# A two-layer hybrid encoder trunk: operands at equal addresses modulo 512 bytes, and the transposes of token blocks 0 and 1 moved to the end of each stage's tail

## The chip, the cores and the metric

The kernel runs on one core of one Trainium2 chip. The metric is the device time of one execution in microseconds, the median of three.

## The reference

Two layers work on 512 tokens of width 1024 in float32. Each layer is three sub-layers, each with an RMSNorm before it and one after it. What matters here:

```python
def swiglu(x, w_gate, w_up, w_down):
    return (jax.nn.silu(x @ w_gate) * (x @ w_up)) @ w_down
...
    for l in range(DEPTH):
        f = swiglu(rms_norm(x, ffn1_pre_g[l]), ...)        # 1024 -> 2816 -> 1024
        x = x + 0.5 * rms_norm(f, ffn1_post_g[l])
        m = hybrid_mixer(rms_norm(x, mix_pre_g[l]), ...)   # in-projection, MLA | GLA | retention, out-projection
        x = x + rms_norm(m, mix_post_g[l])
        f = swiglu(rms_norm(x, ffn2_pre_g[l]), ...)
        x = x + 0.5 * rms_norm(f, ffn2_post_g[l])
```

## The kernel before, in words

**Stages.** There are six stages: FFN, mixer, FFN in each layer, numbered 0 to 5 (`stage % 3 == 1` is a mixer). The program is written per engine, each engine in its own order, with semaphores between them. TensorE (PE) does the matmuls, ScalarE (ACT) and VectorE (DVE) prepare operands and evacuate, GpSimd (POOL) computes inverse roots, SyncE (SP) issues the loads of weights.

**Three matmuls for one.** For accuracy, each float32 operand is split in a high part (rounded to float32r by ACT) and a low part (the rest, by DVE). `three` (L405 to L408) multiplies high by high (L406), high by low (L407), low by high (L408).

**Weights.** They come as a stream of 1 MB "pairs" (two 128-row slabs): 33 for an FFN (`FFN_PAIRS`; 22 for gate and up, 11 for down; `FT` is 22), 12 for a mixer. SP loads pair p into `raw[:, p % 2]` once pair p-2 has been split. ACT's `high` or `high_next` (L838, L853) writes the high part into a slot, DVE's `lows` (L1125) the low part. `slot_of` says which slot: 0 and 1 are halves of `WH`/`WL`, 2 is `WH2`/`WL2`, 3 to 5 are `W3` to `W5`, which lie over `hL`. `high` waits until the slot's last user on PE is done (`pair_done`).

**Which operand is held.** Of a matmul's two operands one is loaded into the array (held, 128 columns), the other streams through (moved, 256 or 512 columns). In gate, up and in-projections a weight tile is held and `xH`/`xL` (the normed, transposed x) moves. In the down and out-projections a piece of `hH`/`hL` (or `xH`/`xL`) is held and the weights move.

**Addresses.** Tiles follow each other in each partition. `x`, `xH`, `xL`, `raw`, `WH`, `WL`, `WH2`, `WL2` start at 128 modulo 512 bytes. Behind a row of small tiles comes `small_end`, 32 bytes, and after it start `hH` and `hL`, and over them `norm_g`, `step`, `xn`, `squares`, `W4`, `W3`, `W5` and the mixer's tiles: the named ones at 0 modulo 512. Steps within all of these are multiples of 512 bytes.

**A tail and the next entry.** An FFN's down projection runs pair by pair over all 8 output tiles (`down_pair`), except for its last three pairs: `last_pairs` goes by token block b (128 tokens, two PSUM banks 2b and 2b+1), and within it over the three pairs n = 0, 1, 2, so that block 0 is complete after a quarter of these 144 matmuls; this stretch is called the tail here. The mixer's out-projection ends in the same way. For each block that is complete, the other engines go through a chain: ACT squares and sums the output (`square_f`, L861), DVE adds (`average_f`, L1144), POOL takes the inverse root (L1476), DVE scales and adds the residual (`residual`, L1153, L1155), ACT squares x (`square_x`, L873), DVE and POOL again (L1160, L1476), DVE writes the normed block to `xn` (`normed`, L1169), PE transposes it (`turn_block`, L418, eight transposes into banks 2b and 2b+1), ACT writes `xH` (`high_x`, L878) and DVE `xL` (`low_x`, L1174). The order in which ACT and DVE take these steps for the four blocks is written out in their two `enter` functions. PE's `turn_block` calls for blocks 0 and 1 stand inside the tail, ahead of n = 1 of b = 2 and b = 3. The next stage begins with `half_pair`: the first pair and the second pair over tokens 0 to 255 (which needs `xH` and `xL` of blocks 0 and 1), with the transposes of blocks 2 and 3 inside, and then both over tokens 256 to 511.

Of the kernel before, what the change touches and what calls it, by code (L numbers as in the profile page):

```python
# [21 lines left out]
P = 128  # L22
# [5 lines left out]
FT = FF // P  # L28
# [14 lines left out]
FFN_PAIRS = FT + FT // 2  # L43
# [5 lines left out]
STAGES = 3 * DEPTH  # L49
# [47 lines left out]


def slot_of(stage, i):
    if i < 2:  # L100
        return 2 + i
    if stage % 3 == 1:
        return {10: 4, 11: 5}.get(i, i % 2)
    return 4 if i == FFN_PAIRS - 1 else i % 2


def first_pair_of(stage):
# [4 lines left out]
def hybrid_trunk(nc, x_in, positions, stream, gains_in, norm_gains, w_q_up, w_kv_up, w_gate_up, b_gate, consts, out):  # L112
    ctx = ExitStack()
    with ctx:
        def sb(name, shape, dt=F32, stack=ctx):
            return stack.enter_context(nc.sbuf_tensor(name, shape, dt))
# [60 lines left out]
        share = sb("share", [P, 2, BLK])  # L177


        sb("small_end", [P, 8])  # L180
        with ExitStack() as hidden:
            hH = sb("hH", [P, FT, SEQ], F32R, hidden)
            hL = sb("hL", [P, FT, SEQ], F32R, hidden)
# [75 lines left out]
        pair_done = sem("pair_done", 0)  # L259
# [139 lines left out]
        def _(pe):  # L399
# [34 lines left out]
            def enter(stage, base, widths=(P, P)):  # L434

                if stage == 0:
                    turn_block(0, 0)
                    turn_block(0, 1)
                wait_pair(base)
                pe.wait_ge(xH_ready, BLK * stage + 2)  # L440
                pe.wait_ge(xL_ready, BLK * stage + 2)
                lower = half_pair(2, (0, 1), 0, (P, P), {})
                if stage:

                    lower.then_inc(pair_done, 1)
                wait_pair(base + 1)
                half_pair(3, (2, 3), 0, widths, {1: (stage, 2), 3: (stage, 3)})
                pe.wait_ge(xH_ready, BLK * stage + 4)
                pe.wait_ge(xL_ready, BLK * stage + 4)
                half_pair(2, (0, 1), 1, (P, P), {}).then_inc(pair_done, 1)  # L450
                half_pair(3, (2, 3), 1, widths, {}).then_inc(pair_done, 1)

            for layer in range(DEPTH):
                due = counter(layer)
# [33 lines left out]
                def last_pairs(stage, p, slots, held):  # L488

                    for b in range(BLK):  # L490
                        for n in range(3):
                            if b == 0:
                                wait_pair(p + n)
                            if b >= 2 and n == 1 and stage < STAGES - 1:
                                turn_block(stage + 1, b - 2)
                            for d in (2 * b, 2 * b + 1):
                                last = down_tile(slots[n], d, held[n], False, n == 2)
                                if n == 2:
                                    last.then_inc(f_ready, 1)
                                elif d == 2 * BLK - 1:  # L500
                                    last.then_inc(pair_done, 1)

                def ffn(stage, f_stage, base):
                    n0 = FT * f_stage
                    enter(stage, base)
                    tiles_pair(base + 2, 0, (4, 5))
                    with pe.Fori(0, (FT - 4) // ROUND_F) as i:
                        for j in range(ROUND_F):
                            f = ROUND_F * i + 3 + j

                            pe.wait_ge(h_ready, n0 + f - 2)
                            tiles_pair(base + f, (1 + j) % 2, FFN_BANKS[j % 3])
                    pe.wait_ge(h_ready, n0 + FT - 3)
                    tiles_pair(base + FT - 1, 1, (0, 1))

                    def hidden(f):
                        pe.wait_ge(hH_ready, n0 + f + 2)
                        pe.wait_ge(hL_ready, n0 + f + 2)
                        return [(hH[:, f + a, :], hL[:, f + a, :]) for a in range(2)]

                    down_pair(base + FT, 0, hidden(0), True, order=FFN_START, emptied=n0 + FT)
                    for n in range(1, 8):
                        down_pair(base + FT + n, n % 2, hidden(2 * n), False)
                    last_pairs(stage, base + FT + 8, (0, 1, 4), (hidden(16), hidden(18), hidden(20)))

                def mixer(stage, base):
                    def pair(i, banks, **kw):
# [291 lines left out]
        def _(act):  # L819
# [3 lines left out]
            for layer in range(DEPTH):  # L823
# [56 lines left out]
                def enter(stage, base):  # L880
                    if stage == 0:
                        square_x(0, 0)
                        square_x(0, 1)
                        high_next(0, base, 0)
                        high_x(0, 0)
                        high_x(0, 1)
                        square_x(0, 2)
                        square_x(0, 3)
                        high_next(0, base, 1)
                        high_x(0, 2)  # L890
                        high_x(0, 3)
                        high_next(0, base, 2)
                    else:
                        high_next(stage, base, 0)
                        high_next(stage, base, 1)
                        square_f(stage, 0)
                        square_x(stage, 0)
                        square_f(stage, 1)
                        square_x(stage, 1)
                        high_x(stage, 0)  # L900
                        square_f(stage, 2)
                        square_x(stage, 2)
                        high_x(stage, 1)
                        square_f(stage, 3)
                        high_next(stage, base, 2)
                        square_x(stage, 3)
                        high_x(stage, 2)
                        high_x(stage, 3)
                    high_next(stage, base, 3)

                def hidden(n, f, p, banks, first=False):

                    act.wait_ge(pair_done, p + 1)
# [6 lines left out]
                def ffn(stage, f_stage, base):  # L920
                    n0 = FT * f_stage
                    enter(stage, base)
                    hidden(n0, 0, base, (0, 1), first=f_stage == 0)
                    hidden(n0 + 1, 1, base + 1, (2, 3))
                    high_at(base, 4)
                    hidden(n0 + 2, 2, base + 2, (4, 5))
                    with act.Fori(0, (FT - 4) // ROUND_F) as i:
                        for j in range(ROUND_F):
                            f = ROUND_F * i + 3 + j
                            high(base + 2 + f, (base + 5 + j) // 2 + ROUND_F // 2 * i, (base + 5 + j) % 2, (1 + j) % 2,  # L930
                                 base + 1 + f)
                            hidden(n0 + f, f, base + f, FFN_BANKS[j % 3])
                    high_at(base, FT + 1)
                    hidden(n0 + FT - 1, FT - 1, base + FT - 1, (0, 1))
                    with act.Fori(1, FT // 4) as m:
                        for j in range(2):
                            high(base + FT + 2 * m + j, (base + FT + j) // 2 + m, (base + FT + j) % 2, j,
                                 base + FT + 2 * m + j - 1)

                    high(base + FT + 10, (base + FT + 10) // 2, (base + FT + 10) % 2, 4, base + FT + 4)  # L940

                def mixer(stage, base):
                    enter(stage, base)
# [7 lines left out]
                    act.dma_start(wq[:, 0, :], w_q_up[layer, 0]).then_inc(mix_landed, 16)  # L951
                    act.dma_start(wq[:, 1, :], w_q_up[layer, 1]).then_inc(mix_landed, 16)
                    act.dma_start(wkv[:], w_kv_up[layer]).then_inc(mix_landed, 16)
                    act.wait_ge(angle_ready, due(angle_ready, 1))
                    af(cos[:], sin[:], ACT.Sin, scale=0.5).then_inc(sine_ready, 1)
                    act.wait_ge(sine_ready, due(sine_ready, 1))
# [150 lines left out]
        def _(dve):  # L1107
# [5 lines left out]
            for layer in range(DEPTH):  # L1113
# [62 lines left out]
                def enter(stage, base):  # L1176
# [12 lines left out]
                        normed(0, 3)  # L1189
                    else:  # L1190
                        low_at(stage, base, 0)
                        low_at(stage, base, 1)
                        average_f(stage, 0)
                        residual(stage, 0)
                        average_x(stage, 0)
                        normed(stage, 0)
                        average_f(stage, 1)
# [13 lines left out]
                    low_x(stage, 2)  # L1211
                    low_x(stage, 3)
                    low_at(stage, base, 2)
                    low_at(stage, base, 3)

                def hidden(n, f, banks, first=False):

# [9 lines left out]
                def ffn(stage, f_stage, base):  # L1227
                    n0 = FT * f_stage
                    enter(stage, base)
                    hidden(n0, 0, (0, 1), first=f_stage == 0)  # L1230
                    hidden(n0 + 1, 1, (2, 3))
                    low_at(stage, base, 4)
                    hidden(n0 + 2, 2, (4, 5))
# [4 lines left out]
                            hidden(n0 + f, f, FFN_BANKS[j % 3])  # L1238
                    low_at(stage, base, FT + 1)
                    hidden(n0 + FT - 1, FT - 1, (0, 1))  # L1240
                    with dve.Fori(1, FT // 4) as m:
                        for j in range(2):
                            lows(base + FT + 2 * m + j, (base + FT + j) % 2, j)
                    low_at(stage, base, FT + 10)

                def mixer(stage, base):
                    enter(stage, base)
                    if layer == 0:
                        dve.wait_ge(gains_landed, 16)

# [405 lines left out]
```

## Time and profile before

| | us |
|---|---|
| median of 3 runs (2038.3 to 2039.79) | 2039.73 |
| the profiled execution's own time | 2042.04 |
| span of its trace | 2040.0 |
| PE busy | 1992.6 (98%) |
| DVE busy | 750.2 (37%) |
| ACT busy | 628.6 (31%) |
| POOL busy | 112.4 (6%) |
| mean granted TensorE clock (1 is full speed) | 0.993 |

Busy time of PE is modelled: pipelined matmuls overlap, so how fast PE goes is read from the distance between the starts of matmuls, and where it stands still from its waits.

### The profile page before, as it was taken

Reading aid. Unit: us, or ns where it says so; the run is one execution under the profiler, and the core shown is the slowest. Engines: PE = TensorE matmul, PEld = TensorE weight load, DVE = VectorE, ACT = ScalarE, POOL = GpSimd, SP = SyncE. Lnnn points to the kernel's source line nnn. Section 1 sums busy time; section 2 is a strip of 40 time slices with the busy share of each in tenths; the row PEclk is TensorE's granted clock in tenths of the full one; section 3 lists DMA queues with packets and bytes.
Section 4 is the critical chain, followed back from the end, with each engine's and each line's share of the span. In section 5 each row is a group of like instructions: output and inputs, shape, how many; then the busy total and the mean of one; then the engine's idle time right before and its main releaser. Section 6 shows DMA issues by size and latency. Waiting matters only on the chain. (4 is left out here: it accounts for less than half of the span.)

```text
span 2040.0 us, 23896 instructions
## 1 busy us (share of the span) xinstructions
PE 1992.6 (98%) x10008; PEld 1634.8 (80%) x10008; DVE 750.2 (37%) x879; ACT 628.6 (31%) x864; POOL 112.4 (6%) x172
## 2 busy tenths in 40 slices
PE   7999999999999999999999999999999999999998
PEld 6888887896678888888798888878966788888886
DVE  4233322634445333332443332225354462333313
ACT  4222212424444222221232222123244542222211
POOL 0000000002230000000000000000022300000000
PEclk9999999999999999999999999999999999999999
DMA  4222232321012222222312222323100122222221
GB/s 177 83 103 91 95 114 93 118 95 42 1 45 101 83 99 86 103 102 105 124 42 103 103 83 103 120 107 128 66 21 1 62 91 96 93 92 103 92 104 62
DMA packets 27349, 180.18 MB, mean 88 GB/s; under 512 B 3298, under 2 KB 3460, under 8 KB 7300
## 3 DMA queue, kind: packets, MB, share of 16 engines
q1 hardware_dynamic: 25760, 174.15, 23.7%
q10 hardware_dynamic: 1508, 4.87, 0.7%
q8 instruction: 61, 1.00, 0.2%
q14 instruction: 20, 0.16, 0.0%
HBM read 176.91 MB, written 2.10 MB: 88 GB/s over the span
## 5 line engine op out<-in xcount | busy, mean ns | idle before, releaser
L1125 DVE TENSOR_TENSOR WL<-raw,WH 128x2048 fp32r<-128x2048 f32 x138 | 315.7, 2291 | 842.2 <-ACT WH L838 818.0
L406 PE MATMUL ps<-xH,WH 128*128 128x512 f32 (+1 forms) x1600 | 604.7, 378 | 3.0 <-DVE xL L1174 3.0
L408 PE MATMUL ps<-xH,WL 128*128 128x512 f32 (+1 forms) x1600 | 602.8, 377 | 0.0
L407 PE MATMUL ps<-xL,WH 128*128 128x512 f32 (+1 forms) x1600 | 602.7, 377 | 0.0
L838 ACT ACTIVATE WH<-raw 128x2048 fp32r<-128x2048 f32 x124 | 237.7, 1917 | 740.3 <-PE ps L408 740.3
L406 PEld LDWEIGHTS ps<-xH,WH 128*128 128x128 f32 x1600 | 301.8, 189 | 59.2 <-issue 4.2
L407 PEld LDWEIGHTS ps<-xL,WH 128*128 128x128 f32 x1600 | 301.8, 189 | 55.3 <-issue 1.0
L408 PEld LDWEIGHTS ps<-xH,WL 128*128 128x128 f32 x1600 | 301.7, 189 | 55.1
L406 PE MATMUL ps<-WH,hH 128*128 128x512 f32 x640 | 254.7, 398 | 6.5 <-DVE WL L1125 6.5
L408 PE MATMUL ps<-WH,hL 128*128 128x512 f32 x640 | 253.7, 396 | 0.0
L407 PE MATMUL ps<-WL,hH 128*128 128x512 f32 x640 | 253.6, 396 | 0.0
L406 PEld LDWEIGHTS ps<-WH,hH 128*128 128x128 f32 x640 | 121.5, 190 | 35.9 <-ACT W L838 8.1
L408 PEld LDWEIGHTS ps<-WH,hL 128*128 128x128 f32 x640 | 121.2, 189 | 28.6
L407 PEld LDWEIGHTS ps<-WL,hH 128*128 128x128 f32 x640 | 121.4, 190 | 28.1
L918 ACT ACTIVATE hH<-up 128x512 f32 (+1 forms) x88 | 55.6, 632 | 211.6 <-DVE up L1222 211.6
L1476 POOL TENSOR_TENSOR rstd_f<-mean_f,minus_half 128x1 f32<-128x1 f32 x24 | 13.2, 550 | 1504.7 <-DVE mean_f L1144 1504.7
L1225 DVE TENSOR_TENSOR hL<-up,hH 128x512 f32 (+1 forms) x88 | 61.0, 693 | 77.9 <-ACT hH L918 77.9
L1222 DVE TENSOR_TENSOR up<-gate,ps 128x512 f32<-128x512 f32 x88 | 59.9, 681 | 27.1 <-ACT gate L916 27.1
L916 ACT ACTIVATE gate<-ps 128x512 f32<-128x512 f32 x88 | 50.8, 577 | 34.9 <-PE ps L408 34.9
L1021 ACT ACTIVATE prob<-ps,minus_top 128x128 f32<-128x128 f32 (+1 forms) x64 | 33.8, 528 | 77.9 <-DVE minus_top L1417 77.9
L406 PE MATMUL ps<-xH,W 128*128 128x256 f32 x192 | 55.0, 286 | 0.0
L408 PE MATMUL ps<-xH,W 128*128 128x256 f32 x192 | 54.0, 281 | 0.0
(211 smaller groups left out, 1941.2 us busy)
## 6 DMA issues: line engine op xcount, KB each, us to landing
raw<-stream SPq DMA_DIRECT2D x156, 1024.0 KB, 4.8
norm_g<-norm_gains SPq DMA_DIRECT2D x12, 512.0 KB, 5.3
x<-x_in SPq DMA_DIRECT2D x4, 512.0 KB, 8.4
wq<-w_q_up ACTq DMA_DIRECT2D x4, 512.0 KB
out<-x SPq DMA_DIRECT2D x4, 512.0 KB, 2.6
const<-consts ACTq DMA_DIRECT2D x2, 578.5 KB
wkv<-w_kv_up ACTq DMA_DIRECT2D x2, 512.0 KB
cos<-positions ACTq DMA_DIRECT2D x2, 256.0 KB
```

The source lines that it names most:

```text
L406: mm(dst, wh, xh, start=start, stop=False)
L407: mm(dst, wh, xl, start=False, stop=False)
L408: return mm(dst, wl, xh, start=False, stop=stop)
L838: af(wH(slot), raw[:, raw_slot, :], ACT.Copy).then_inc(wH_ready, 1)
L916: af(gate[:], ps[:, banks[0], :], ACT.Silu).then_inc(silu_ready, 1)
L918: af(hH[:, f, :], up[:], ACT.Copy).then_inc(hH_ready, 1)
L1021: af(prob[:, m % 3, 0:width], ps[:, RING[m % 4], 0:width], ACT.Exp, scale=QK ** -0.5, bias=minus_top[:, m % 4:m % 4 + 1], accum_out=total[ ...
L1125: tt(wL(slot), raw[:, raw_slot, :], wH(slot).bitcast(F32), ALU.subtract).then_inc(wL_ready, 1)
L1222: tt(up[:], gate[:], ps[:, banks[1], :], ALU.mult).then_inc(h_ready, 1)
L1225: tt(hL[:, f, :], up[:], hH[:, f, :].bitcast(F32), ALU.subtract).then_inc(hL_ready, 1)
L1476: nc.gpsimd.tensor_tensor(to[:, b:b + 1], mean_of[:, b:b + 1], minus_half[:, 0:1], ALU.pow).then_inc(done, 1)
```

## The change

A float32 tile `small_end` becomes 128 bytes longer, so that everything behind it starts at 128 modulo 512 bytes too (`hH`, `hL`, `xn`, `W3` to `W5` among it). In stages other than 2 and 5 the second pair is held in slot 1 and no longer in slot 3; pair 3 (slot 1) is therefore converted after the second pair's last matmul. In an FFN the last three pairs lie in slots 0, 4, 3 instead of 0, 1, 4. PE's transposes of blocks 0 and 1 stand behind the tail. ACT squares block 0 before it converts the next stage's second pair; DVE makes that pair's low part after the residual of block 0.

```diff
 def slot_of(stage, i):
-    if i < 2:
-        return 2 + i
+    if i == 0:
+        return 2
+    if i == 1:
+        return 3 if stage % 3 == 2 else 1
     if stage % 3 == 1:
         return {10: 4, 11: 5}.get(i, i % 2)
-    return 4 if i == FFN_PAIRS - 1 else i % 2
+    return {FFN_PAIRS - 2: 4, FFN_PAIRS - 1: 3}.get(i, i % 2)
...
-        sb("small_end", [P, 8])
+        sb("small_end", [P, 40])
...
@@ tensor: enter (twice), last_pairs, ffn @@
-                half_pair(3, (2, 3), 0, widths, {1: (stage, 2), 3: (stage, 3)})
+                half_pair(slot_of(stage, 1), (2, 3), 0, widths, {1: (stage, 2), 3: (stage, 3)})
...
                             if b == 0:
                                 wait_pair(p + n)
-                            if b >= 2 and n == 1 and stage < STAGES - 1:
-                                turn_block(stage + 1, b - 2)
...
+                    if stage < STAGES - 1:
+                        turn_block(stage + 1, 0)
+                        turn_block(stage + 1, 1)
...
-                    last_pairs(stage, base + FT + 8, (0, 1, 4), (hidden(16), hidden(18), hidden(20)))
+                    last_pairs(stage, base + FT + 8, (0, 4, 3), (hidden(16), hidden(18), hidden(20)))
...
@@ scalar: enter, ffn, mixer @@
                         high_next(stage, base, 0)
+                        square_f(stage, 0)
                         high_next(stage, base, 1)
-                        square_f(stage, 0)
                         square_x(stage, 0)
...
-                    high_next(stage, base, 3)
...
                     hidden(n0, 0, base, (0, 1), first=f_stage == 0)
+                    high_at(base, 3)
                     hidden(n0 + 1, 1, base + 1, (2, 3))
...
-                    with act.Fori(1, FT // 4) as m:
+                    with act.Fori(1, FT // 4 - 1) as m:
...
-                    high(base + FT + 10, (base + FT + 10) // 2, (base + FT + 10) % 2, 4, base + FT + 4)
+                    for i, slot, done in ((FT + 8, 0, FT + 7), (FT + 9, 4, FT + 4), (FT + 10, 3, FT + 8)):
+                        high(base + i, (base + i) // 2, (base + i) % 2, slot, base + done)
...
                     act.dma_start(wkv[:], w_kv_up[layer]).then_inc(mix_landed, 16)
+                    high_at(base, 3)
+
                     act.wait_ge(angle_ready, due(angle_ready, 1))
...
@@ vector: enter, ffn, mixer @@
                         low_at(stage, base, 0)
-                        low_at(stage, base, 1)
                         average_f(stage, 0)
                         residual(stage, 0)
+                        low_at(stage, base, 1)
                         average_x(stage, 0)
...
                     low_at(stage, base, 2)
-                    low_at(stage, base, 3)
...
```

DVE's `low_at(3)` moves to the same places as ACT's `high_at(3)`: behind the first `hidden` in an FFN, right behind `enter` in a mixer.

**PE, the end of stage 0's tail.** `xn` is the normed block that L418 (L420 after) transposes. Before, at token block 2, pair n = 1:

```order
L406 MATMUL ps<-WH,hH 128x512
L407 MATMUL ps<-WL,hH 128x512
L408 MATMUL ps<-WH,hL 128x512
L418 MATMUL ps<-ident,xn 128x128 [waits xn_ready]
L418 MATMUL ps<-ident,xn 128x128 x7
L406 MATMUL ps<-WH,hH 128x512
```

Now, at the tail's last tile:

```order
L408 MATMUL ps<-W,hH 128x512
L409 MATMUL ps<-W,hH 128x512
L410 MATMUL ps<-W,hL 128x512
L420 MATMUL ps<-ident,xn 128x128 [waits xn_ready]
L420 MATMUL ps<-ident,xn 128x128 x7
L420 MATMUL ps<-ident,xn 128x128 [waits xn_ready]
L420 MATMUL ps<-ident,xn 128x128 x7
L408 MATMUL ps<-xH,WH 128x256 [waits xH_ready,xL_ready,wL_ready,wH_ready]
```

Between block 1's transposes and the next stage's first matmul, which waits for `xH` and `xL` of both blocks, PE has no other work; before, 24 of the tail's matmuls stood behind block 1's transposes.

**ACT, from the last pair of stage 0 to the second `high_x` of stage 1.** L853 is `high_next`, L861 `square_f`, L873 `square_x`, L878 `high_x` (after: L856, L864, L876, L881). Before:

```order
L838 ACTIVATE W<-raw 128x2048 [waits pair_done,pair_landed0]
L853 ACTIVATE WH<-raw 128x2048 [waits hL_ready,pair_landed1]
L853 ACTIVATE W<-raw 128x2048 [waits f_ready,pair_landed0]
L861 ACTIVATE squares,sum_f<-ps 128x512 [waits f_ready] x2
L873 ACTIVATE squares,sum_x<-x 128x1024 [waits x_ready]
L861 ACTIVATE squares,sum_f<-ps 128x512 [waits sum_f_ready,f_ready] x2
L873 ACTIVATE squares,sum_x<-x 128x1024 [waits sum_x_ready,x_ready]
L878 ACTIVATE xH<-ps 128x8x128 [waits x_turned]
L861 ACTIVATE squares,sum_f<-ps 128x512 [waits sum_f_ready,f_ready] x2
L873 ACTIVATE squares,sum_x<-x 128x1024 [waits sum_x_ready,x_ready]
L878 ACTIVATE xH<-ps 128x8x128 [waits x_turned]
```

Now:

```order
L841 ACTIVATE W<-raw 128x2048 [waits pair_done,pair_landed0]
L856 ACTIVATE WH<-raw 128x2048 [waits hL_ready,pair_landed1]
L864 ACTIVATE squares,sum_f<-ps 128x512 [waits f_ready] x2
L856 ACTIVATE WH<-raw 128x2048 [waits f_ready,pair_landed0]
L876 ACTIVATE squares,sum_x<-x 128x1024 [waits x_ready]
L864 ACTIVATE squares,sum_f<-ps 128x512 [waits sum_f_ready,f_ready] x2
L876 ACTIVATE squares,sum_x<-x 128x1024 [waits sum_x_ready,x_ready]
L881 ACTIVATE xH<-ps 128x8x128 [waits x_turned]
L864 ACTIVATE squares,sum_f<-ps 128x512 [waits sum_f_ready,f_ready] x2
L876 ACTIVATE squares,sum_x<-x 128x1024 [waits sum_x_ready,x_ready]
L881 ACTIVATE xH<-ps 128x8x128 [waits x_turned]
```

The squares of block 0 moved ahead of the second pair's conversion. The rest kept its order: the squares of block 2's output and of its x still stand between the two `high_x`.

## Rows read from the trace of the kernel before

**Rows 1.** The page, busy time and share of the span by engine
```profile
PE 1992.6 (98%) x10008; PEld 1634.8 (80%) x10008; DVE 750.2 (37%) x879; ACT 628.6 (31%) x864; POOL 112.4 (6%) x172
```
**Rows 2.** Waits of PE over the span: us in total, times, longest
```profile
PE ps L418 <- DVE xn L1169: 21.6, 5, 11.8
...
PE ps L406 <- DVE WL L1125: 6.5, 4, 1.6
```
**Rows 3.** Windows of five tails: us, PE, PEld, DVE, ACT, POOL busy, PEclk, DMA
```profile
351.34:390.38 39.04, 35.52 (x161) 28.56 (x160) 23.39 (x21) 17.19 (x26) 3.30 (x6) 1.00 0.29 108
619.13:656.13 37.00, 35.21 (x162) 28.56 (x160) 21.82 (x21) 13.68 (x25) 3.32 (x6) 1.00 0.32 114
987.60:1030.91 43.31, 38.27 (x161) 30.80 (x160) 23.48 (x21) 17.19 (x26) 3.30 (x6) 0.92 0.28 98
1362.40:1403.85 41.45, 37.15 (x161) 29.82 (x160) 23.49 (x21) 17.20 (x26) 3.30 (x6) 0.96 0.28 102
1630.88:1665.98 35.10, 35.10 (x162) 28.56 (x160) 21.83 (x21) 13.70 (x25) 3.32 (x6) 1.00 0.33 120
```
**Rows 4.** Line L406 on PE: count, ns min/median/max, first to last start, form
```profile
L406 PE MATMUL ps<-WH,hH x127: 390/393/404, 262.1 to 349.9; 128*128 128x512 f32 x127
...
L406 PE MATMUL ps<-xH,WH x265: 389/389/389, 60.1 to 239.7; 128*128 128x512 f32 x133
...
L406 PE MATMUL ps<-xH,WH x16: 282/283/283, 390.4 to 395.8; 128*128 128x256 f32 x16
...
L406 PE MATMUL ps<-xH,W x16: 274/281/283, 409.3 to 414.6; 128*128 128x256 f32 x8, 128*112 128x256 f32 x8
```
**Rows 5.** Timeline of PE at a tail's end (start, length), nine neighbours' first and last
```profile
388.34 0.39 PE L406 MATMUL ps<-W,hH 128*128 128x512 f32 x1
...
390.15 0.40 PE L408 MATMUL ps<-W,hL 128*128 128x512 f32 x1
```
**Rows 6.** Timeline of the chain of blocks 0 to 2 into stage 1
```profile
396.84 1.03 PE L418 MATMUL ps<-ident,xn 128*128 128x128 f32 x8
397.91 1.03 ACT L878 ACTIVATE xH<-ps 128x1024 fp32r<-128x1024 f32 x1 [2.05 <-PE ps L418]
...
379.04 1.00 ACT L878 ACTIVATE xH<-ps 128x1024 fp32r<-128x1024 f32 x1
...
372.44 0.58 ACT L861 ACTIVATE squares<-ps 128x512 f32<-128x512 f32 x1
...
373.49 0.20 ACT L861 ACTIVATION_READ_ACCUMULATOR squares<-ps 128x1 f32 x1
...
382.31 0.15 DVE L1144 SCALAR_TENSOR_TENSOR mean_f<-sum_f 128x1 f32<-128x1 f32 x1
...
385.70 1.06 ACT L873 ACTIVATE squares<-x 128x1024 f32<-128x1024 f32 x1 [3.61 <-DVE x L1155]
...
386.76 1.01 ACT L878 ACTIVATE xH<-ps 128x1024 fp32r<-128x1024 f32 x1
...
387.80 1.22 DVE L1174 TENSOR_TENSOR xL<-ps,xH 128x1024 fp32r<-128x1024 f32 x1 [0.76 <-ACT xH L878]
```
**Rows 7.** Timeline of the program's start: last `xL` of blocks 0, 1, then PE
```profile
15.79 2.35 DVE L1174 TENSOR_TENSOR xL<-ps,xH 128x1024 fp32r<-128x1024 f32 x2
...
18.29 0.54 PE L406 MATMUL ps<-xH,WH 128*128 128x256 f32 x1 [3.04 <-DVE xL L1174]
```
**Rows 8.** Windows after three stops of PE, columns as in rows 3
```profile
18.30:21.70 3.40, 3.40 (x16) 3.40 (x17) 1.44 (x2) 2.09 (x3) 1.08 (x2) 0.50 0.54 229
...
1012.50:1018.40 5.90, 5.89 (x18) 5.01 (x19) 3.32 (x5) 2.06 (x3) 1.10 (x2) 0.50 0.00 0
...
1386.50:1390.50 4.00, 3.93 (x15) 3.36 (x16) 2.60 (x4) 0.67 (x1) 0.55 (x1) 0.57 0.00 0
```
**Rows 9.** DVE splits stage 0's second-last pair; the page's loads of pairs, median landing
```profile
353.49 2.29 DVE L1125 TENSOR_TENSOR WL<-raw,WH 128x2048 fp32r<-128x2048 f32 x1 [8.86 <-ACT WH L838]
...
raw<-stream SPq DMA_DIRECT2D x156, 1024.0 KB, 4.8
```

More of the change, by code:

```diff
@@ L450, in enter @@
                 half_pair(2, (0, 1), 1, (P, P), {}).then_inc(pair_done, 1)
-                half_pair(3, (2, 3), 1, widths, {}).then_inc(pair_done, 1)
+                half_pair(slot_of(stage, 1), (2, 3), 1, widths, {}).then_inc(pair_done, 1)
             for layer in range(DEPTH):
@@ L1230, in ffn @@
                     hidden(n0, 0, (0, 1), first=f_stage == 0)
+                    low_at(stage, base, 3)
                     hidden(n0 + 1, 1, (2, 3))
@@ L1240, in ffn @@
                     hidden(n0 + FT - 1, FT - 1, (0, 1))
-                    with dve.Fori(1, FT // 4) as m:
+                    with dve.Fori(1, FT // 4 - 1) as m:
                         for j in range(2):
                             lows(base + FT + 2 * m + j, (base + FT + j) % 2, j)
-                    low_at(stage, base, FT + 10)
+                    for i in range(8, 11):
+                        low_at(stage, base, FT + i)
                 def mixer(stage, base):
                     enter(stage, base)
+                    low_at(stage, base, 3)
                     if layer == 0:
```

## The prediction

> **What bounds the kernel now.** I read the page first: PE is busy for 98% of the span, no other engine for 40% [rows 1]. So the time is PE's work at the rate at which it goes, plus PE's stops. Then the waits of PE: it stops ahead of the transposes of `xn` (21.6 us in five places, 11.8 of them the program's start) and four times, once per FFN, for a low half of a pair, 6.5 us together [rows 2]. These stops lie in the tails. I marked each of the five tails that another stage follows, from its first of 144 matmuls to the next stage's first matmul: they take 39.0, 37.0, 43.3, 41.5 and 35.1 us [rows 3], together **195.9 us**. A window less its PE busy time, less 1.6 for the low half where the stage is an FFN (the first, third and fourth), leaves the stop ahead of the transposes: 1.9, 1.8, 3.4, 2.7 and 0 us. Last, the rate, from the starts of line L406, which is every third matmul. In the down projection 127 of them lie between 262.1 and 349.9, so one matmul starts every 87.8/(126x3) = 0.2323 us; in gate and up 265 lie between 60.1 and 239.7, which gives 179.6/(264x3) = 0.2268 us [rows 4]. Both move 512 columns.
>
> **Part 1, equal addresses.** In gate and up, both operands start at 128 modulo 512 bytes; in the down projection the held one (`hH`) starts at 0 and the moved one (`WH`) at 128. That this relation is what costs the 5.5 ns, and not which tensor is held, can be read in one place: the tail's last pair lies in `W4`, at 0 like `hH`, and there nine matmuls start from 388.34 to 390.15, one every 0.2263 us [rows 5], with the same roles. Now all of these start at 128, and I expect 0.2268 everywhere. Outside the five tails that is 4 FFNs x 8 pairs x 48 matmuls = 1536, and 96 in the last stage's tail (the third of its pairs is equal already): 1632 x 5.5 ns = **-9.0 us**. The five tails are worked out whole in part 3, at the new rate. The second pair of each entry is unequal too (W3 with `xH`), but its 256-column matmuls start every 5.3/45 = 0.118 us and the equal first pair's every 5.4/45 = 0.120 [rows 4]; 6 x 96 of them at 2 ns more are **+1 us**. The other matmuls whose addresses move (transposes and small ones of the attention) keep or change their relation without a row that tells a price; I take nothing, between -1 and +1.
>
> Here the Trainium skill speaks against the change. "SBUF — State Buffer", section "Who interferes with whom", gives PE two independent read ports, one for the moved operand and one for weight loads, and says that only a port pair shared by VectorE and GpSimd causes contention; by that rule the operands' addresses would change nothing, and part 1 would be worth zero. The rows speak for a difference; the rule's case is a rival below.
>
> **Part 2, slots.** The tail's second pair waits in an FFN because slot 1 only comes free when the tail begins: DVE ends its low half at 353.49 + 2.29 = 355.78, 4.4 us into the tail [rows 3, 9]. In slot 4, free since the fourth pair of the down projection, it is ready before the tail: this stop goes, 6.5/4 = 1.6 us, **-1.6 us** for the last stage (the others are in part 3). What is late next is the third pair, now in slot 3, which is free only as the tail begins: it is ready 4.4 us into the tail, and PE wants it after 24 matmuls, at 24 x 0.2268 = 5.4 us. It is covered by 1 us. Its raw data follow the low half of the pair two before, which ends some 6.4 us ahead of the tail (the same 4.4 us after the start of the pair before it, which takes 48 matmuls, 10.9 us); at 4.8 us a load [rows 9] they are there. Pair 3 of each stage is now converted after the second pair's last matmul, in the same 4.4 us, beside pair 2's 48 matmuls or 10.9 us: nothing. In the mixer DVE's copies of the first banks queue behind it, some 4.4 + 2.7 us, still inside those 10.9.
>
> **Part 3, the transposes at the tail's end.** The tail's matmuls now run without a stop: 144 x 0.2268 = 32.65 us. `xn` of blocks 0 and 1 is ready by then (block 0's squares no longer wait for the second pair's conversion). After that PE transposes and has nothing until `xL` of block 1. The order on ACT decides how long: `high_x(0)` waits for the transposes, and everything behind it with it. Between the two `high_x` stand block 2's squares, which need DVE's residual of block 2, which needs `sum_f` of block 2. So a chain that lay beside the tail is now behind it. Step by step [rows 6]:
>
> - transposes of block 0 to the start of `high_x`: 397.91 - 396.84 = 1.07
> - `high_x(0)`: 1.00
> - `square_f(2)`, both halves: 373.49 + 0.20 - 372.44 = 1.25
> - sum, inverse root, scale, residual, until `square_x(2)` starts: 385.70 - 382.31 = 3.39
> - `square_x(2)`: 386.76 - 385.70 = 1.06
> - `high_x(1)` and the hand-over to DVE: 387.80 - 386.76 = 1.04
> - `low_x(1)`: 1.22
> - DVE's end to PE's first matmul: 18.29 - 18.14 = 0.15 [rows 7]
>
> That is 10.2 us; the 16 transposes cover 1.8 of it, so PE stands still for 8.4 us, five times. A tail becomes 32.65 + 10.2 = 42.85 us, five of them 214.3, against 195.9: **+18.4 us**. The blocks 2 and 3 come after the same start as now, with the same distances, and find PE in the first pair.
>
> **Part 4, the clock.** After each of three stops, of 3.0 us [rows 7], 3.4 and 2.7 (above), PE ran at a granted clock of 0.5, that is 1.2 instead of 2.4 GHz: for 3.4 us at the program's start, 5.9 us from 1012.5, and in the third at 0.57 over 4.0 us, so some 3.4 us [rows 8]. In the tails with stops of 1.9 us and less the clock stayed at 1.00 [rows 3]. A stop of 8.4 us is longer than all of these, so all five entries begin at 0.5. The price for 256-column matmuls: 16 of them in 3.4 us where 16 x 0.12 = 1.9 would do, 1.5 us; for 5.9 us in proportion 2.6. I take 2.1, in the middle, since one low stretch was long and two short: 5 x 2.1 = **+10.5 us**, between 7.5 and 13. What the two low stretches of before cost is in the 195.9 already.
>
> The Trainium skill agrees in direction: "TensorE: Matmul & The Clock Gate", section "Why this matters for your kernels", asks for no long idle gaps between bursts of matmuls, because the array falls back to its low clock. By that rule this change is a bad one at five places; the rows above give it its price.
>
> **The sum.** -9.0 + 1 - 1.6 + 18.4 + 10.5 = **+19.3 us**. It is made against the profiled execution: span 2040.0, its own time 2042.04, which lies 2.3 us above the median of the runs. Added to the median of 2039.73, it gives **2059 us**. A measurement of this kernel tells about 0.2%, 4 us, from no change.
>
> **The rivals.**
>
> - *The clock stays up* (or rises at once). For it: after the stops of 1.9 us nothing fell. Against: all three longer ones were followed by 0.5. Without part 4 it is +8.8, **2048.5 us**. 7%.
> - *The addresses are worth nothing*, the skill's rule above. For it: the equal matmuls of the down projection are few and stand in tails alone. Against: same roles, same engines beside them, and yet 0.2263. Then part 1's -9.0 goes, and five tails take 144 x 5.5 ns = 0.8 more each: +32.3, **2072 us**. 8%.
> - *A new wait in the tail or in the entry*: the third pair is covered by 1 us only. If its data land 2 to 3 us late, or the mixer's copies hold a pair, it is 1 to 2 us in four to six places: **2064 to 2068 us**. 8%.
> - *Faster, 2022 to 2032 us.* The stop is only as long as at the program's start, where between the last transposes and the first matmul lie 3.0 us [rows 7]. This would be so if block 2's chain had run before block 0 was transposed; the point from which it decides is whether block 2's squares stand ahead of the first `high_x` on ACT. Then a tail takes 32.65 + 1.8 + 3.0 = 37.45, five 187.3, -8.6; with parts 1 and 2 it is -18.2, 2022, with five short stretches at the low clock, 5 x 1.5, some 2029, 2032 where they are longer. Against it: ACT's order is fixed, with `high_x(0)` first. 5%.
> - *The change does not do what it says*: the second FFN waits vanish but the stops are hidden by something I missed, and all of it cancels, **2036 to 2044 us**. 3%.
>
> **How the numbers follow.** The forecast has 69%. The predicted time is its own, 2059. Its terms leave 2055 to 2063; the range reaches to the clock rival below and to the late pair above, 2049 to 2068, and leaves out the addresses' rival, the two fast cases and the edge of the first. Faster by over 0.2% has 6%, the fast rival and a part of the last; within 0.2% 2%; slower 92%.
>
> **What the profile would show.** Right: in five places PE's wait for `xL` (L1179 after), 8 to 9 us each, none for `xn` and none for a low half in the tail; five windows of some 43 us; after each a clock of 0.5 for 3 to 6 us; L408 in the down projection one start in 0.2268 us. Wrong: a stop near 3 us (block 2's chain was not in the way), a clock of 1.0 right after it, 0.232 in the down projection, or a wait of PE for `W3`'s low half 5.4 us into an FFN's tail.

## The result, and the profile after

The changed kernel takes **2061.36 us** (median of 4, 2060.92 to 2061.65) against 2039.01 before in the same comparison: ratio 1.011, with a 95% interval of 1.0092 to 1.0127. It is slower, as forecast, and within the range; 2059 was predicted. The profiled executions have spans of 2059.4 and 2040.0, a difference of 19.4 us; the sum had said 19.3.

The page (busy time) and PE's waits, after:

```profile
PE 1987.4 (97%) x10008; PEld 1643.6 (80%) x10008; DVE 749.5 (36%) x879; ACT 628.4 (31%) x864; POOL 112.3 (5%) x172
```
```profile
PE ps L408 <- DVE xL L1179: 44.0, 6, 8.2
PE ps L420 <- DVE xn L1174: 11.8, 1, 11.8
```

The waits for `xn` inside the tails and for the low half [rows 2] are gone. In their place PE waits for `xL`, six times: 2.8 us at the program's start and 8.2 us ahead of each of the five entries.

The windows of the five tails, cut as in [rows 3], after (us, then busy time of PE, PEld, DVE, ACT, POOL, then granted clock and DMA):

```profile
350.13:392.92 42.79, 34.56 (x161) 28.67 (x160) 20.16 (x20) 16.32 (x28) 3.29 (x6) 0.95 0.22 79
622.61:665.40 42.79, 34.55 (x161) 28.68 (x160) 20.78 (x21) 14.68 (x28) 3.31 (x6) 0.96 0.28 99
996.40:1039.18 42.78, 34.55 (x161) 28.67 (x160) 20.25 (x20) 16.27 (x28) 3.29 (x6) 0.94 0.21 79
1370.91:1413.70 42.79, 34.55 (x162) 28.68 (x160) 20.17 (x20) 16.45 (x28) 3.29 (x6) 0.95 0.23 80
1645.03:1687.81 42.78, 34.55 (x161) 28.67 (x160) 20.77 (x21) 14.67 (x28) 3.31 (x6) 0.94 0.27 99
```

All five are 42.8 us, FFN and mixer alike, where before they went from 35.1 to 43.3: one chain sets all of them. It can be read on ACT and DVE in the timeline of the first (start, length, ..., idle before and who ended it):

```profile
383.85 1.02 ACT L881 ACTIVATE xH<-ps 128x1024 fp32r<-128x1024 f32 x1 [11.93 <-PE ps L420]
384.77 0.59 ACT L864 ACTIVATE squares<-ps 128x512 f32<-128x512 f32 x1
...
389.46 1.06 ACT L876 ACTIVATE squares<-x 128x1024 f32<-128x1024 f32 x1 [3.43 <-DVE x L1160]
...
390.52 1.00 ACT L881 ACTIVATE xH<-ps 128x1024 fp32r<-128x1024 f32 x1
```
```profile
386.89 1.28 DVE L1158 SCALAR_TENSOR_TENSOR step<-ps,rstd_f,norm_g 128x1024 f32<-128x1024 f32 x1 [0.66 <-POOL rstd_f L1483]
388.20 1.22 DVE L1160 TENSOR_TENSOR x<-x,step 128x1024 f32<-128x1024 f32 x1
...
391.55 1.22 DVE L1179 TENSOR_TENSOR xL<-ps,xH 128x1024 fp32r<-128x1024 f32 x1 [0.76 <-ACT xH L881]
```

ACT had stood idle for 11.93 us ahead of its first `high_x`, with block 2's squares queued behind it; they and the residual run only now, while PE waits. DVE's order holds the same chain back: `low_x(0)` stands ahead of `average_f(2)` there, and DVE idled for 10.85 us in front of it:

```profile
384.91 1.23 DVE L1179 TENSOR_TENSOR xL<-ps,xH 128x1024 fp32r<-128x1024 f32 x1 [10.85 <-ACT xH L881]
```

The first half pair of each entry, 48 matmuls of 256 columns (same columns; granted clock is the third number from the end):

```profile
392.93:399.98 7.05, 7.05 (x48) 7.05 (x49) 4.47 (x6) 2.70 (x3) 1.10 (x2) 0.80 0.00 0
665.40:672.73 7.33, 7.33 (x49) 7.33 (x49) 4.75 (x6) 2.70 (x3) 1.10 (x2) 0.77 0.01 2
1039.20:1047.24 8.04, 8.04 (x48) 8.04 (x49) 5.05 (x6) 2.69 (x3) 1.10 (x2) 0.69 0.00 0
1413.70:1422.16 8.46, 8.46 (x48) 8.46 (x49) 5.06 (x6) 2.70 (x3) 1.10 (x2) 0.64 0.00 0
1687.80:1695.83 8.03, 8.01 (x48) 8.03 (x49) 5.08 (x6) 2.72 (x3) 1.10 (x2) 0.69 0.01 2
```

At the full clock each takes 48 x 0.120 = 5.8 us [rows 4]; the five take 38.9, so 10.1 us more. Ahead of the first entry the clock had fallen while PE still stood, a mean of 0.74 over the stop, so that part of the low stretch cost nothing:

```profile
384.90:393.30 8.40, 0.38 (x2) 0.41 (x3) 5.72 (x7) 4.97 (x12) 1.10 (x2) 0.74 0.00 0
```

And the down projection, line L408 of stage 0 (count, ns min/median/max, first to last start):

```profile
L408 PE MATMUL ps<-WH,hH x128: 389/389/389, 263.1 to 349.5; 128*128 128x512 f32 x128
```

One matmul starts every 86.4/(127 x 3) = 0.2268 us, against 0.2323 [rows 4]. The eight pairs ahead of stage 0's tail, 384 matmuls, before and after:

```profile
262.11:351.34 89.23, 89.23 (x385) 72.33 (x384) 19.63 (x10) 16.45 (x10) 0.00 (x0) 1.00 0.30 106
```
```profile
263.10:350.13 87.03, 87.03 (x385) 72.07 (x384) 21.83 (x11) 18.25 (x11) 0.00 (x0) 1.00 0.33 119
```

That is 2.2 us less, and the same in the other three FFNs: 8.8 us. The last stage's tail, before and after:

```profile
1997.51:2032.70 35.19, 33.56 (x145) 26.78 (x143) 12.49 (x11) 8.54 (x16) 1.65 (x3) 1.00 0.11 46
```
```profile
2019.50:2052.14 32.64, 32.64 (x145) 26.84 (x143) 10.30 (x10) 6.72 (x15) 1.64 (x3) 1.00 0.12 49
```

### The profile page after: what moved, and what is told of

Its sections match the earlier page's. It is cut to its first block, busy times and chain, and to the rows that moved or that the text cites. A ratio compares the mean times of both kernels' runs of the same rounds, so it can differ in the third digit from the quotient of the medians.

```text
span 2059.4 us, 23867 instructions
## 1 busy us (share of the span) xinstructions
PE 1987.4 (97%) x10008; PEld 1643.6 (80%) x10008; DVE 749.5 (36%) x879; ACT 628.4 (31%) x864; POOL 112.3 (5%) x172
## 4 chain that ended last, share of the span: by engine, by line
PE 93%; DVE 2%; ACT 2%; issue 1%; POOL 1%; DMA 0%; SPq 0%; POOLq 0%; ACTq 0%; DVEq 0%
PE ps L408 27%; PE ps L410 27%; PE ps L409 27%; PE ps L727 2%; PE ps L620 1%; PE ps L745 1%; PE ps L541 1%; PE ps L542 1%; PE ps L543 1%; PE ps L420 1%; DVE xL L1179 1%; PE ps L734 1%; PE ps L629 1%; ACT xH L881 0%; PE ps L672 0%
## 5 line engine op out<-in xcount | busy, mean ns | idle before, releaser
L408 PE MATMUL ps<-xH,WH 128*128 128x512 f32 (+1 forms) x1728 | 647.2, 375 | 44.0 <-DVE xL L1179 44.0
L409 PE MATMUL ps<-xL,WH 128*128 128x512 f32 (+1 forms) x1728 | 643.6, 372 | 0.0
L410 PE MATMUL ps<-xH,WL 128*128 128x512 f32 (+1 forms) x1728 | 643.5, 372 | 0.0
L408 PEld LDWEIGHTS ps<-xH,WH 128*128 128x128 f32 x1728 | 331.2, 192 | 100.8 <-issue 46.4
L409 PEld LDWEIGHTS ps<-xL,WH 128*128 128x128 f32 x1728 | 331.0, 192 | 55.2 <-issue 1.0
L410 PEld LDWEIGHTS ps<-xH,WL 128*128 128x128 f32 x1728 | 330.7, 191 | 55.5
L408 PE MATMUL ps<-WH,hH 128*128 128x512 f32 x576 | 224.1, 389 | 0.0
L409 PE MATMUL ps<-WL,hH 128*128 128x512 f32 x576 | 224.1, 389 | 0.0
L410 PE MATMUL ps<-WH,hL 128*128 128x512 f32 x576 | 224.1, 389 | 0.0
L408 PEld LDWEIGHTS ps<-WH,hH 128*128 128x128 f32 x576 | 108.1, 188 | 22.2
L1179 DVE TENSOR_TENSOR xL<-ps,xH 128x1024 fp32r<-128x1024 f32 x24 | 29.3, 1224 | 82.9 <-ACT xH L881 82.9
L881 ACT ACTIVATE xH<-ps 128x1024 fp32r<-128x1024 f32 x24 | 24.5, 1021 | 95.6 <-PE ps L420 95.6
```

The costliest lines, as they stand in the source:

```text
L408: mm(dst, wh, xh, start=start, stop=False)
L409: mm(dst, wh, xl, start=False, stop=False)
L410: return mm(dst, wl, xh, start=False, stop=stop)
L1179: tt(block_of(xL, b), turned_block(b), block_of(xH, b).bitcast(F32), ALU.subtract).then_inc(xL_ready, 1)
```

## The experiments

Times are medians; "before" in a ratio is the kernel before, run on the same chip beside each.

**The transposes alone.** The kernel before, with this edit:

```diff
-                            if b >= 2 and n == 1 and stage < STAGES - 1:
-                                turn_block(stage + 1, b - 2)
...
+                    if stage < STAGES - 1:
+                        turn_block(stage + 1, 0)
+                        turn_block(stage + 1, 1)
```

> The kernel before with one edit: PE's transposes of blocks 0 and 1 stand behind the tail. Addresses, slots and the order on ACT and DVE are those of before. If the chain of block 2 between the two high_x sets the stop, each tail is its matmuls (33.2 us, with 1.8 more in an FFN for the late low half) and 10.2 us: 45.2 in three and 43.2 in two, 222 against 195.9, +26; with some 10 us of low clock behind five stops it is +36, about 2075 us. If the transposes' place alone cost little and the rest of the change was what made it slow, it stays within 10 us of before.

Measured: 2078.34 us, ratio 1.0205 (1.0188 to 1.0222), some 42 us more. Two of its five windows, an FFN's and a mixer's tail:

```profile
352.07:397.42 45.35, 35.49 (x162) 28.62 (x160) 22.46 (x21) 17.80 (x29) 3.30 (x6) 0.94 0.25 93
625.10:668.47 43.37, 35.13 (x161) 28.61 (x160) 20.91 (x21) 14.30 (x28) 3.32 (x6) 0.97 0.27 97
```

45.4 and 43.4 us, as expected to 0.2. The place of the transposes is the whole loss; the other parts of the change pay some of it back. The profiled spans differ by 35.2 us, which is the forecast; the medians by 6 more (the interval is 38 to 45). Those 6 us lie in the two profiled executions: that of before (2042.04, granted clock 0.993) is 4.9 us above the median of the runs of before beside this one (clock 0.995 to 0.997), that of this kernel 1.3 below its own.

**The change without it.** The changed kernel, with that edit undone:

> The changed kernel with one edit undone: the transposes of blocks 0 and 1 are back ahead of n = 1 of token blocks 2 and 3. Equal addresses, slots and the order on ACT and DVE stay as changed. My theory: no stop at all in the tails (xn of block 0 is ready some 17 us into a tail, PE wants it at 19), so a tail is 32.65 + 1.8 = 34.5 instead of 42.8, five times -41.7, and the low clock behind the stops goes too, -10: about 2010 us, faster than both kernels. If PE still waits for xn of block 0 by 1 to 2 us, 2015 to 2020.

Measured: **2007.49 us**, ratio 0.9857 (0.9840 to 0.9873): 29 us below before and the fastest of all. Three of its tails and PE's longest waits:

```profile
348.91:383.36 34.45, 34.45 (x162) 28.68 (x161) 21.19 (x20) 15.72 (x25) 3.31 (x6) 1.00 0.27 99
608.59:643.04 34.45, 34.45 (x161) 28.68 (x160) 21.79 (x21) 14.08 (x25) 3.33 (x6) 1.00 0.35 123
972.47:1006.92 34.45, 34.45 (x162) 28.68 (x160) 21.19 (x20) 15.73 (x25) 3.30 (x6) 1.00 0.27 97
```
```profile
PE ps L420 <- DVE xn L1173: 11.4, 1, 11.4
PE ps L744 <- ACT probT L1034: 4.2, 6, 1.2
PE ps L408 <- DVE xL L1178: 3.4, 1, 3.4
```

Each tail is its matmuls and transposes and PE is busy for all of it. The two waits for `xn` and `xL` are the program's start.

**Slots and order alone.** The same, and `small_end` as before:

```diff
-        sb("small_end", [P, 40])
+        sb("small_end", [P, 8])
```

> The changed kernel with the transposes back in the tail and small_end as before: what is left of the change is the slots and the order on ACT and DVE. If these remove both kinds of stop in the tails (the late low half, 1.8 us in four, and the wait for xn, 1.9 to 3.5 us in four of five), each tail is its matmuls and transposes, 33.3 + 1.8 = 35.1, five 175.5 against 195.9, and the last one 1.8 shorter: about 22 us below before. The down projection stays at 0.2323 us a matmul, so it is 10 to 12 us above the kernel that has the equal addresses too. If the stops only moved, it is less than 12 below before.

Measured: 2020.18 us, ratio 0.9905 (0.9875 to 0.9935), 13 to 26 us below before. The stops are gone here too; what is missing against the kernel above is the rate of the down projection:

```profile
L408 PE MATMUL ps<-WH,hH x125: 390/393/404, 263.3 to 349.7; 128*128 128x512 f32 x125
```

86.4/(124 x 3) = 0.2323 us, as before; over 2112 matmuls at 5.5 ns that is 11.6 of the 12.7 us.

**Addresses alone.** The kernel before, with `small_end` of 40 instead of 8 columns.

> The kernel before with small_end 128 bytes longer and nothing else. If the relation of the two operands' addresses is what costs 5.5 ns, one matmul of 512 columns starts every 0.2268 us in the down projection too, and 2112 matmuls save 11.6 us, less about 1 for the second pairs: 2028 to 2029 us. If PE's two reads never meet, whatever their addresses, the distance stays 0.2323 and the time 2039.

Measured: 2030.53 us (10 runs, 2025.44 to 2036.4), ratio 0.9964 (0.9950 to 0.9978), so 4 to 10 us less, somewhat below the forecast. The rate came as expected:

```profile
L406 PE MATMUL ps<-WH,hH x111: 389/389/390, 270.1 to 344.9; 128*128 128x512 f32 x111
```

74.8/330 = 0.2267 us. But in the tails that wait for `xn`, PE arrives earlier and waits longer: its wait ahead of block 0's transposes at the end of stage 0 is 2.5 us where it was 1.9. After that stop of 2.5 us the clock fell to 0.5, which it did not after the 1.9 us of before [rows 3]:

```profile
374.70:378.10 3.40, 3.40 (x9) 2.62 (x9) 1.99 (x3) 1.50 (x3) 0.08 (x1) 0.50 0.00 0
```

The shortfall goes with the clock. The ten runs of this kernel have mean granted clocks of 0.990 to 0.996, the thirteen of before beside them 0.995 to 0.997. At 0.996, three of this kernel took 2025.4 to 2027.3 us and five of before 2035.1 to 2038.2; at 0.995, two took 2026.9 and 2028.8 and five 2039.3 to 2041.2. So at the same clock it is 10 to 12 us less, which is the forecast.

**How far apart is far.** The same edit with other lengths moves the held operand to 160, 384 or 64 modulo 512 bytes, the moved one stays at 128.

> The kernel before with small_end 160 bytes longer: in the down projection the held operand starts at 160, the moved one at 128 modulo 512 bytes. If equality modulo 512 is what counts, one matmul starts every 0.232 us as before; if only the distance in 64-byte or 128-byte lines counts, 0.2268.

> The kernel before with small_end 384 bytes longer: held at 384, moved at 128 modulo 512 bytes, equal modulo 256. If the period is 512 bytes, one matmul in the down projection every 0.232 us or more; if it is 256 or less, 0.2268. Over 0.232 would say that the price grows with the distance.

> The kernel before with small_end 64 bytes longer: held at 64, moved at 128 modulo 512 bytes. If any inequality costs the same, 0.232; if the price goes with the distance, between 0.2268 and 0.2323.

Line L406 in the down projection of the first, the second and the third:

```profile
L406 PE MATMUL ps<-WH,hH x108: 395/396/396, 270.0 to 344.9; 128*128 128x512 f32 x108
```
```profile
L406 PE MATMUL ps<-WH,hH x111: 389/389/389, 270.0 to 344.8; 128*128 128x512 f32 x111
```
```profile
L406 PE MATMUL ps<-WH,hH x109: 392/392/393, 270.2 to 344.3; 128*128 128x512 f32 x109
```

Distances of 32 bytes cost 74.9/321 = 0.2333, more than the 128 bytes of before. At 256 bytes it is 74.8/330 = 0.2267: as good as equal. So equality modulo 512 bytes is not needed; on these distances, equality modulo 256 is enough. At 64 bytes it is 74.1/324 = 0.2287, between the two. Single runs of 2044.5, 2035.9 and 2033.0 us; each says little by itself.

The same traces tell whether it is the relation or `hH`'s own place. In a tail's last pair both operands lie behind `small_end`, so they start at equal addresses in every one of these kernels. Seven starts in the first run's, both at 160:

```profile
368.35 0.39 PE L406 MATMUL ps<-W,hH 128*128 128x512 f32 x1
...
369.71 0.40 PE L406 MATMUL ps<-WH,hH 128*128 128x512 f32 x1
```

1.36/6 = 0.2267 us, where the unequal matmuls of the same run have 0.2333; with both at 64 it is 0.2267 too (359.98 to 361.34 us). So it is the relation. But this rate comes only at the end of each dozen of such matmuls, after some three to ten slower ones, where the matmuls ahead of them were unequal; why it takes so long was not tried.

**ACT's order.** The changed kernel with its transposes at the tail's end, and on ACT (on DVE likewise):

```diff
-                        high_x(stage, 0)
                         square_f(stage, 2)
                         square_x(stage, 2)
+                        high_x(stage, 0)
                         high_x(stage, 1)
```

> The changed kernel with another order on ACT and DVE: block 2's squares and residual ahead of the first high_x, both high_x and both low_x in a row behind it. The transposes stay at the tail's end. If it is ACT's order that makes the stop 8.4 us, it falls to 3.0 us as at the program's start: five tails of 37.4 instead of 42.8, -27; the clock behind stops of 3 us stays low for less or equally long, 0 to -3: 2031 to 2034 us. If the stop is set by something else (the transposes' own latency, POOL), it stays above 6 us and the time above 2050.

Measured: 2024.76 us, ratio 0.9946 (0.9930 to 0.9963), 7 to 14 us below before. PE's waits, the program's start (2.8 us) among them:

```profile
PE ps L408 <- DVE xL L1179: 16.4, 6, 2.8
```

The five entries wait (16.4 - 2.8)/5 = 2.7 us in place of 8.2, so it is the order on ACT and DVE that makes the stop. The two were moved together, and neither alone was tried; in the changed kernel both hold the chain back. I had expected 2031 to 2034. The clock fell in three of the five entries only: their first half pairs take 33.6 us together, 5.3 less than in the changed kernel. Two of them:

```profile
652.82:658.65 5.83, 5.83 (x48) 5.83 (x49) 3.78 (x5) 2.49 (x3) 0.60 (x2) 1.00 0.01 3
1019.59:1026.92 7.33, 7.32 (x49) 7.33 (x49) 4.75 (x6) 2.49 (x3) 1.10 (x2) 0.77 0.00 0
```

**The clock's share.** The changed kernel, with superfluous matmuls of PE in the stop, into bank 0, which the entry's first matmul overwrites:

```diff
+                        wait_pair(first_pair_of(stage + 1))
+                        pe.wait_ge(xH_ready, BLK * (stage + 1) + 1)
+                        pe.wait_ge(xL_ready, BLK * (stage + 1) + 1)
+                        for i in range(56):
+                            mm(ps[:, 0, 0:P], wH(2)[:, 0:P], xH[:, 0, 0:P], start=True, stop=True)
```

> The changed kernel, and in each of the five stops PE does 56 superfluous matmuls of 128 columns into bank 0 once block 0's xL is there (their result is overwritten by the entry's first matmul). They fill the stop from some 3.5 us after its tail on and delay nothing, so the stop ahead of the first useful matmul stays 8.4 us long and only the clock can change. If the low clock behind the stops costs 10 us, the entries run at 1.00, each first half pair takes 5.8 us instead of 7.1 to 8.5, and the kernel is 10 us faster than the changed one, some 12 above before. If the slow start of the entries is not the clock's, it stays 22 above before. If the 56 end late, by 0.1 us each beyond 6.5, it shows as a later first half pair.

Measured: 2067.06 us, in runs from 2055 to 2080: this one did not do what it was made for. The four runs follow their mean granted clock, from 0.992 at 2055 to 0.979 at 2080. The windows while the 56 run, in the first and in the last of the five entries:

```profile
385.50:386.90 1.40, 1.40 (x15) 1.40 (x14) 1.37 (x2) 0.00 (x0) 0.00 (x0) 1.00 0.00 0
386.90:394.60 7.70, 7.70 (x39) 7.70 (x38) 5.03 (x7) 5.01 (x8) 1.10 (x2) 0.50 0.01 2
...
1694.20:1700.80 6.60, 6.43 (x56) 6.29 (x56) 3.99 (x5) 3.42 (x8) 1.10 (x2) 1.00 0.00 0
```

PE had stood for 1.6 us and then did matmuls of 128 columns without a break. The clock fell all the same, to 0.5, in four of the five; the matmuls took twice as long and the entry came late. In the last it did not fall. So the next two have matmuls of 512 columns, `mm(ps[:, 0, :], xH[:, 0, 0:P], wH(2)[:, 0:SEQ], ...)`, 24 of them; the first of the two also repeats block 1's transposes.

> As the filler before, but with 24 superfluous matmuls of 512 columns in place of 56 of 128, and block 1 transposed three times over ahead of the signal, so that PE has something to do for nearly all of each stop (1.7 us more of transposes, 24 x 0.227 = 5.5 us of matmuls, in 8.4 us). If it is PE's missing work that lets the clock fall behind the stops, it stays at 1.00 in all five entries, each first half pair takes 5.8 us, and the kernel is 10 us faster than the changed one, some 12 above before; the stop up to the first useful matmul stays as long as it was. If the clock falls all the same, 18 to 30 above before.

> The same 24 superfluous matmuls of 512 columns, without the repeated transposes: PE stands still for 1.9 us, works for 5.5 and waits for 1 more. If a stop of 1.9 us is harmless, as ahead of the transposes in two tails of before, it comes out as the full filler, some 12 above before. If work after a 1.9 us stop comes too late in some entries, the clock falls in those, the 24 take 0.427 each and the entry is up to 4 us late: 14 to 30 above before, with a wide spread over the runs.

Measured: 2047.96 us, ratio 1.0043 (1.0026 to 1.0059), and 2049.38 us, 1.0050 (1.0031 to 1.0069). The first half pairs of the full filler, three of five:

```profile
391.96:397.78 5.82, 5.82 (x48) 5.82 (x49) 3.78 (x5) 2.70 (x3) 0.59 (x2) 1.00 0.01 3
664.92:670.75 5.83, 5.82 (x48) 5.83 (x49) 3.79 (x5) 2.71 (x3) 0.60 (x2) 1.00 0.01 3
1037.21:1043.03 5.82, 5.82 (x48) 5.82 (x49) 3.78 (x5) 2.71 (x3) 0.59 (x2) 1.00 0.01 3
```

All five are at the full clock, 5.8 us instead of 7.1 to 8.5, and the first useful matmul still comes 8.2 us behind the first pass of the transposes. It is the same without the repeated transposes, where PE stands for 1.6 us as with the first filler; the first of its five:

```profile
391.60:397.42 5.82, 5.82 (x49) 5.82 (x50) 3.75 (x5) 2.68 (x3) 0.62 (x2) 1.00 0.01 3
```

The half pairs are 9.8 us shorter than in the changed kernel. By the ratios the two kernels lie 9 and 10 us above before (5 to 12, 6 to 14) where the changed one lies 22 (19 to 26): the clock's share is 12 to 14 us, which these intervals do not tell from the 10 expected. Work that computes nothing earns it back.

## Why the prediction was right, point by point

| term | predicted, us | from the profiles, us |
|---|---|---|
| five tails (part 3) | +18.4 | 213.9 - 195.9 = +18.0 |
| low clock at the entries (part 4) | +10.5 | 38.9 - 28.8 = +10.1 |
| down projections outside the tails (part 1) | -8.4 | 4 x (87.0 - 89.2) = -8.8 |
| last tail (parts 1 and 2) | -0.6 - 1.6 = -2.2 | 32.6 - 35.2 = -2.5 |
| second pairs (part 1) | +1 | 0 |
| the program's first half pair | 0 | 8.2 - 7.3 = +0.9 |
| the two mixers behind their entries' half pairs | 0 | -0.3 + 1.6 = +1.3 |
| not placed | | +0.4 |
| sum | +19.3 | 2059.4 - 2040.0 = +19.4 |

The mechanism came as forecast: the chain, the stop, the low clock behind it and the rate. That the two sums agree to 0.1 us is luck: the terms that were off and those that were left out cancel. The two mixers took 228.8 and 227.0 us from entry to tail before and 229.7 and 231.3 after, of which 1.3 and 2.7 are the slow half pairs; what makes the other 1.6 in the second was not isolated.

- *The chain* (part 3) was put at 10.2 us from the tail's end, 8.4 of them a stop. All five windows came out at 42.8 us against 42.85, with a stop of 8.2. That the place of block 2's squares decides was the point of the fast rival, which named ACT's order alone; DVE's holds the chain too. Moving both cut the wait to 2.7 us and brought 2025 us, between that rival's 2022 without the low clock and 2029 with it behind all five. The rival's condition was the right one as far as it went; the kernel as changed did not meet it.
- *The clock* (part 4) was sized from three stretches at 0.5. The average was right, 2.0 us each against 2.1, and the sum lies inside 7.5 to 13; single entries (1.3 to 2.7) spread a little wider than the 1.5 to 2.6 taken from the rows. The reading that stops of 1.9 us and less do no harm held for that trace. It is no safe bound: the clock fell behind a stop of 1.6 us in four of the 128-column filler's entries. The rule of the Trainium skill cited there ("TensorE: Matmul & The Clock Gate", section "Why this matters for your kernels"), no long idle gaps between bursts of matmuls, agrees with the trace for the stops of 8.2 us, all five followed by 0.5.
- *The addresses* (part 1): 0.2267 us in the down projections of all four FFNs. The forecast was read from nine matmuls, and there was luck in which: they are the settled end of their dozen, while the same pair's first dozen in stage 2's tail, at equal addresses too, runs from 995.04 to 997.59 in the kernel before, one start every 0.232 us. The rival of the two independent read ports falls; the measurement decides against the Trainium skill's rule here ("SBUF — State Buffer", section "Who interferes with whom"). The change's own reading, modulo 512, is stricter than what the runs show. The +1 us for the second pairs did not come: an entry's 192 matmuls and 16 transposes take 24.5 to 24.6 us before and 24.4 to 24.6 in the changed kernel with its transposes in the tail.
- *The slots* (part 2): no late low half any more; the third pair, with 1 us of cover, was never late.
- *What was off*: against the medians the change is +22.4 us, 3 more than the sum. The profiled execution of before (2042.04) lies 3.0 us above its median, that of the changed kernel (2061.50) 0.1 above, so the comparison of spans flatters the change by those 3 us. The distance goes with the clock: over all runs of before on record, those with a mean granted clock of 0.993 took 2040.6 to 2044.3 us, those with 0.997 took 2033.3 to 2037.7, and the profiled one has 0.993. The changed kernel, whose long stops all end at the low clock, has 0.985 in every run and a spread of 0.7 us. I had seen most of that distance and then set the sum on the median without allowing for it; on the profiled execution's own time it would have given 2042.0 + 19.3 = 2061.3.

## What to carry to other kernels

Move a producer of a chain later only after reading the in-order queues that wait for it: here two of PE's small steps moved by some 14 and 5 us (60 and 24 matmuls), and what they blocked on ACT and DVE was the next block's whole chain. A stop of the matmul engine can cost twice, its length and the low clock after it: here 8.2 and some 2 us, five times. Where a large matmul stream runs a few ns slower in one phase than in another with the same shapes, compare the start addresses of the two operands; here 128 bytes of padding gave 5.5 of 232 ns.

## What the runs showed of the hardware that I had not expected

- In this stream of float32r matmuls of 512 columns one starts every 0.2267 us when the held and the moved operand start at equal addresses modulo 256 bytes (distances 0 and 256), every 0.2323 at 128, every 0.2333 at 32 and every 0.2287 at 64. Why 64 lies between was not tried, nor any other distance. Equal ones that follow unequal ones reach 0.2267 only after some three to ten matmuls.
- The granted clock fell to 0.5 after a stop of 1.6 us that 128-column matmuls followed, in four of five places, and in none of five where 512-column matmuls followed the same stop. After stops of 2.7 us it fell in three of five entries, and after one of 2.5 us in the kernel with the addresses alone. So whether a short stop costs anything differs from place to place in one execution.
